# A two-block transformer kernel on one core: norms by token halves, unread products at the opening and in the last norm, and low halves sooner

## The reference, cut to what matters

```
first_block:  h = rmsnorm(x);  proj = h @ w_in             # compressed, selected, window attention
              mix = concat(o_nsa, o_swa) @ w_o
              x = x + rmsnorm(mix)                         # "y1": the norm behind w_o
              h = rmsnorm(x);  y = (gelu(conv(a)) * u) @ w_down    # a, u = split(h @ w_gate_up)
              x = x + rmsnorm(y)                           # "y2": the norm behind w_down
              x = x + (p @ w_ple) * sigmoid(x @ w_ple_gate)
second_block: proj = rms_norm(x) @ w_in_2
              na  = neighbourhood_attention(q, k, v)       # 8 heads, softmax over a window
              ret = head_group_norm(bidirectional_retention(rotary(q), rotary(k), v))
              x = x + concat(na, silu(g) * ret) @ w_out_2
              x = x + square(relu(rms_norm(x) @ w_up_2)) @ w_down_2
result:       rms_norm(x)                                  # "x5": the last norm
```

## Time and profile before

| | us |
|---|---|
| three runs | 1301.70, 1303.32, 1304.52 |
| median | 1303.32 |
| the profiled execution | 1304.54 |
| its span, first to last instruction | 1302.7 |
| outside of the span | 1.8 |
| mean granted TensorE clock | 0.995 |

### The profile page before, as it was taken

The page is one execution under the profiler, slowest core; times in us unless marked ns, Lnnn a source line. Parts: engine busy times, 40 slices in busy tenths (PEclk is TensorE's granted clock), DMA queues, the critical chain, the costliest instruction groups (busy, mean ns, idle before and its releaser), DMA issues.

```text
span 1302.7 us, 16590 instructions
## 1 busy us (share of the span) xinstructions
PE 1278.1 (98%) x6086; PEld 1062.3 (82%) x6086; DVE 802.3 (62%) x1553; ACT 634.5 (49%) x1239; POOL 155.1 (12%) x146
## 2 busy tenths in 40 slices
PE   8999999999999999999999999999999999999997
PEld 7888888868888888888788777888888888888886
DVE  5789799685654566346788886588644343344344
ACT  6687576454335443233455655476543242332343
POOL 0021120000010001000002101022311030110111
PEclk9999999999999999999999999999999999999998
DMA  7211110423332333332333222432333323233321
GB/s 266 85 46 41 42 41 18 157 76 90 99 97 71 115 104 97 98 90 81 113 90 89 89 57 64 128 105 77 91 96 97 94 76 114 81 113 97 98 81 65
DMA packets 64623, 118.19 MB, mean 91 GB/s; under 512 B 7712, under 2 KB 12192, under 8 KB 64288
## 3 DMA queue, kind: packets, MB, share of 16 engines
q1 hardware_dynamic: 62848, 112.95, 29.2%
q10 hardware_dynamic: 1696, 4.19, 1.0%
HBM read 115.02 MB, written 2.10 MB: 90 GB/s over the span
## 4 chain that ended last, share of the span: by engine, by line
PE 88%; DVE 7%; ACT 2%; issue 2%; DMA 1%; POOL 0%; SPq 0%; POOLq 0%; DVEq 0%; ACTq 0%
PE bank L581 26%; PE bank L583 26%; PE bank L582 25%; PE bank L781 2%; PE bank L662 2%; PE bank L664 2%; PE bank L663 2%; DVE pp L2094 1%; PE bank L767 1%; PE bank L768 1%; DVE ptl L2117 1%; DVE pp L2111 1%; PE bank L735 1%; DMA praw<-in_pT 0%; DVE qs L2010 0%
## 5 line engine op out<-in xcount | busy, mean ns | idle before, releaser
L1923 DVE TENSOR_TENSOR wl<-raw,wh 128x512 fp32r<-128x512 f32 (+2 forms) x360 | 265.9, 750 | 330.8 <-ACT wh L1257 330.1
L1257 ACT ACTIVATE wh<-raw 128x512 fp32r<-128x512 f32 (+1 forms) x398 | 242.3, 619 | 289.6 <-PE bank L583 276.0
L581 PE MATMUL bank<-AH,wh 128*128 128x512 f32 (+1 forms) x848 | 333.5, 393 | 0.9 <-DVE AL L1937 0.3
L583 PE MATMUL bank<-AH,wl 128*128 128x512 f32 (+1 forms) x848 | 329.2, 388 | 0.0
L582 PE MATMUL bank<-AL,wh 128*128 128x512 f32 (+1 forms) x848 | 326.9, 386 | 0.0
L581 PE MATMUL bank<-BH,wh 128*128 128x512 f32 x624 | 247.9, 397 | 1.3 <-DVE wl L1923 1.3
L583 PE MATMUL bank<-BH,wl 128*128 128x512 f32 x624 | 244.7, 392 | 0.0
L582 PE MATMUL bank<-BL,wh 128*128 128x512 f32 x624 | 243.2, 390 | 0.0
L583 PEld LDWEIGHTS bank<-AH,wl 128*128 128x128 f32 x848 | 159.3, 188 | 35.4
L581 PEld LDWEIGHTS bank<-AH,wh 128*128 128x128 f32 x848 | 159.8, 188 | 34.7 <-issue 4.1
L582 PEld LDWEIGHTS bank<-AL,wh 128*128 128x128 f32 x848 | 159.5, 188 | 33.1 <-issue 0.2
(11 more groups left out here) (317 smaller groups left out, 1627.0 us busy)
## 6 DMA issues: line engine op xcount, KB each, us to landing
raw<-in_w_dn SPq DMA_DIRECT2D x104, 256.0 KB, 2.7
raw<-in_w_gu SPq DMA_DIRECT2D x88, 256.0 KB, 2.6
raw<-in_w_up SPq DMA_DIRECT2D x64, 256.0 KB, 2.6
raw<-in_w_nsa SPq DMA_DIRECT2D x16, 256.0 KB, 2.7
raw<-in_w_pg SPq DMA_DIRECT2D x16, 256.0 KB, 2.6
raw<-in_w_naq SPq DMA_DIRECT2D x16, 256.0 KB, 2.6
nbi<-in_na_bias ACTq DMA_DIRECT2D x8, 448.0 KB, 3.4
raw<-in_w_swa SPq DMA_DIRECT2D x10, 256.0 KB, 2.7
```

Source lines behind the costliest of these rows:

```text
L581: t.matmul(o, w, xh, start=start, stop=False, skip_group_check=skip)
L583: return t.matmul(o, wl, xh, start=False, stop=stop, skip_group_check=skip)
L1257: a.activation(W[i % NW].h[:, 0:n], RAW[i % NRAW][:, 0:n], ACT.Copy).then_inc(*s_wh.up(i))
L1923: v.tensor_tensor(w.l[:, 0:n], RAW[i % NRAW][:, 0:n], w.h[:, 0:n], ALU.subtract).then_inc(*s_wl.up(i))
```

## The change

1. Opening. The DMA of `cst` moves from SP's queue to ACT's, as its first instruction. PE begins with eight f32 products of `ones` by `ones`, 128 columns each, into a bank whose content is overwritten and never read. The 12 products of chunk 0 are put in another order, with a wait for each kind: four w.h by x.h (after `AH` and `wh`), four by x.l (after `AL`), four w.l (after `wl`).
2. Norms y1 and y2. The last chunk is added in two halves of 256 tokens (`y1_last`, `y2_last`), squared in two (`squares_by_halves`), and PE's sums of it wait for each half apart. Chunk 0 is scaled, added and split to `AH` in halves (`x1_first`, `x2_first`, `first_split`), and PE's fresh products take half the columns at a time. ACT loads the root's table earlier: in y1 two chunks sooner, in y2 during the last down products. In y1 `behind("w_ple", 0)` moves behind the first chunk's scaling and adding.
3. Retention. On DVE two low halves of `w_ret` (behind 3, ahead 4) move ahead of rotated_low(0) and rotated(1).
4. Neighbourhood attention. On DVE rest(s-2) goes before soft(s) in every round.
5. Last norm. On ACT last_root(0) goes before last_square(6, 1); on DVE last_norm(0) before last_add(6, 1). PE gets three f32 products of `ones` between the two sources of last_sums(1) and six behind it, into a bank of their own, not read.

The diff, cut to its core; products within are shown by their first line where they repeat:

```diff
@@ tokens
+                for n in range(warm):
+                    t.matmul(bs[3][:, 0:P], ones[:, :], ones[:, :], start=True, stop=True)
...
+                    if warm and k == 0:
+                        e.wait_ge(s_xh.at(("x0", 0)), s_wh.at(i))
+                        for b in range(4):
+                            t.matmul(bs[b][:, 0:N], x.h[:, P * b:P * b + P], w.h[:, 0:N], start=True, stop=False)
+                        e.wait_ge(ready(0))
...
+                        e.wait_ge(low(i))
...
@@ product, fresh
-                        e.wait_ge(s_xh.at((fresh, ks[0])))
...
+                        for h in range(2):
+                            o = of_tokens(h)
+                            e.wait_ge(s_xh.at((fresh, ks[0], h)))
...
@@ squares_of
+                    if halves and i % 2 == 0:
+                        e.wait_ge(s_sq.at((key, 7, i // 2)))
@@ last norm on PE
+                    if n and h:
+                        awake(3)
...
             last_sums(1)
+            awake(6)
@@ ACT
+            a.dma_start(cst[:, 0:c_used[0]], ins["consts"]).then_inc(*s_c.up("in", by=16))
...
             for c in range(8):
+                if c == 6:
+                    root_table("y1")
                 hi(WHERE["w_o_nsa", c] + 4)
...
-                if c == 7:
-                    root_table("y1")
-                out1(c)
+                if c < 7:
+                    out1(c)
+            squares_by_halves("y1", chunk(ACC, 7), ("y1", 7))
...
+                        if j == 6:
+                            root_table("y2")
...
-            root_table("y2")
-            down_out(2, 7)
+            squares_by_halves("y2", chunk(ACC, 7), ("dn", 2, 7))
...
+            last_root(0)
             last_square(6, 1)
-            last_root(0)
@@ DVE
+            def x1_first(h):
+                v.scalar_tensor_tensor(out=t[:, o], in0=chunk(ACC, 0)[:, o], ...
+                v.tensor_tensor(chunk(X, 0)[:, o], chunk(X, 0)[:, o], t[:, o], ALU.add)...
...
+            x1_first(0)
+            x1_first(1)
             behind("w_ple", 0)
-            x1_scaled(0)
-            x1_sum(0)
...
-            x2_scaled(0)
-            x2_sum(0)
+            x2_first(0)
+            x2_first(1)
...
             rotated(0)
+            behind("w_ret", 3)
+            ahead("w_ret", 4, 2)
             rotated_low(0)
             rotated(1)
-            behind("w_ret", 3)
-            ahead("w_ret", 4, 2)
...
             for s in range(10):
+                if s >= 2:
+                    u = s - 2
+                    rest(NA, ("na", u), PT2[u % 2], ...
                 if s < 8:
                     soft(NA, ("na", s), PP2[s % 2], ...
-                if s >= 2:
-                    u = s - 2
-                    rest(NA, ("na", u), PT2[u % 2], ...
...
+            last_norm(0)
             last_add(6, 1)
-            last_norm(0)
@@ SP
-            d.dma_start(cst[:, 0:c_used[0]], ins["consts"]).then_inc(*s_c.up("in", by=16))
```

More of the change, by code:

```diff
@@ L583, in triple, with group @@
                 return t.matmul(o, wl, xh, start=False, stop=stop, skip_group_check=skip)
-            def group(name, k, bs, keys, src, ready, ks, first, last):
+            def group(name, k, bs, keys, src, ready, ks, first, last, skip=False):
                 G = len(keys)
@@ L1222, in last_sums, with awake @@
                 bank.give(("st", "x5", h))
+            def awake(n):
+                for _ in range(n):
+                    t.matmul(bank.ap(("awake",))[:, 0:P], ones[:, :], ones[:, :], start=True, stop=True)
             def last_back(name, h):
@@ L1238, in tensor @@
             last_part(7, 1, {(0, 2): lambda: last_back("bk", 0), (1, 0): lambda: last_back("bk2", 0)})
+            b, free = bank.take(("awake",))
+            e.wait_ge(*free)
             last_sums(1)
+            awake(6)
+            bank.give(("awake",))
             last_back("bk", 1)
@@ L1278, in square, with squares_by_halves, first_split @@
                         sqr.read((key, c), (s_st, (key, "c", c)))
+            def squares_by_halves(key, x, done):
+                for h in range(2):
+                    e.wait_ge(s_sv.at((*done, h)), *sqr.before((key, 7)))
+                    a.activation(sqr.ap((key, 7))[:, of_tokens(h)], x[:, of_tokens(h)], ACT.Square).then_inc(*s_sq.up((key, 7, h)))
+                sqr.read((key, 7), (s_st, (key, "c", 7)))
+            def first_split(key, dst, src, scale, *ready):
+                for h in range(2):
+                    o = of_tokens(h)
+                    e.wait_ge((s_sv if key == "x1" else s_dv).at((key, 0, h)), *ready)
+                    if scale is None:
+                        m = a.activation(dst.h[:, o], src[:, o], ACT.Copy)
+                    else:
+                        m = a.activation(dst.h[:, o], src[:, o], ACT.Copy, scale=scale)
+                    m.then_inc(*s_xh.up((key, 0, h)))
             def root(key):
@@ L2248, in y1, with y1_last @@
                 bank.read(key, (s_sv, ("y1", c)))
+            def y1_last():
+                key = ("wo", 7)
+                e.wait_ge(s_mm.at(("o", key)), s_cp.at(("wos", 7)), s_pv.at(N_UNITS - 1))
+                for h in range(2):
+                    o = of_tokens(h)
+                    v.tensor_tensor(chunk(ACC, 7)[:, o], bank.ap(key)[:, o], ACC1[7][:, o], ALU.add).then_inc(*s_sv.up(("y1", 7, h)))
+                bank.read(key, (s_sv, ("y1", 7, 1)))
             for c in range(8):
-                y1(c)
+                if c < 7:
+                    y1(c)
+                else:
+                    y1_last()
                 behind("w_o_nsa", c)
```

94 lines of the change are left out of this document (65 added, 29 removed).

## The result

| | before | changed |
|---|---|---|
| median of 13 runs | 1302.19 | 1305.15 |
| lowest to highest | 1301.50 to 1304.75 | 1302.72 to 1307.27 |
| profiled execution's span | 1302.7 | 1305.5 |

The ratio is 1.0017, with a 95% interval of 1.001 to 1.0025: slower by 2 to 3 us, where I had forecast 1297.2 and given "slower" a chance of 0.04. By my own bound of 0.2% it is "within 0.2%", but it lies outside of the range and on the wrong side of the old kernel.

A forecast was written before the change was run, and what follows sets the result against it. PE, busy 98% of 1302.7 us, was taken as the bound. Terms 2.6 + 2.3 + 0.2 + 1.1 - 1.5 + 2.0 = 6.7 us gave 1297.8 from the profiled run, 1296.6 from the median; forecast 1297.2, range 1293.5 to 1301.0.

The forecast's parts named there:

- Neighbourhood, -1.5 forecast: Neighbourhood attention: values start no sooner, exp 1.6 later, loop 7.4 us against PE's 6.85; loss 1.5, bounds +1.6 and -2.5.
- Carried through the last four rounds ... earlier rounds add some tenths: Neighbourhood attention: the longer loop ends the stage 1.1 us later over four rounds, earlier rounds adding some tenths.
- Rival (d): Neighbourhood rounds, 842 to 905 us: waits lower the clock, 1.7 a fall, six falls giving 1307.4; chance 0.04.
- Opening, 2.6 forecast: Start of kernel: first product at about 5.1, clock up sooner through unread products; gain 2.6 us, bounds 1.3 and 3.1.
- the rise again 5.6 us after the first real product: Opening, lower bound: unread products do nothing for the clock, gain 1.3 us.
- Norm y1, 2.3 forecast: Norm y1: sums end 0.7 sooner and the half clock behind them goes; gain 2.3 us, bounds 0.6 and 2.4.
- If the clock stays up: Norm y1, behind the sums: PE reaches L711 at 266.8, a gain of 2.4 us; if it falls again, 0.7.
- Norm y2, 0.2: Norm y2: sums 0.5 sooner, DVE pays 0.28 more for halves; gain 0.2 us, bounds 0 and 0.5.
- Retention, 1.1 forecast: Retention: PE's wait of 1.31 for `wl` goes entirely; gain 1.1 us, bounds 0.8 and 1.5.
- about 0.5 of room: Retention: rotated low halves come some 0.6 later; products using them, 10 us on, have about 0.5 us of room.
- Last norm, 2.0: Last norm: 1.5 from the wait for identity blocks, 0.5 from spreading at full clock; bounds 1.3 and 2.4.
- the two clock terms: The gains forecast for the opening (2.6) and norm y1 (2.3), together 4.9 of 6.7 us.

The follow-up runs named there:

- b_na_new: The kernel before with only the neighbourhood order changed, rest(s-2) before soft(s): 1309.00 us, ratio 1.0053.
- a_na_late: The changed kernel with rest(s-2) before soft(s) only in neighbourhood rounds 6 to 9, which project nothing: 1298.78 us, ratio 0.9971.
- b_open10: The kernel before with only the opening changed, with ten unread products instead of eight: 1298.95 us, ratio 0.9971.
- a_na_old: The changed kernel with soft(s) before rest(s-2) again in all ten neighbourhood rounds: 1297.79 us, ratio 0.9961.
- n_ret_old: The changed kernel with the neighbourhood order and the retention order undone: 1298.39 us, ratio 0.9967.

## Why the prediction was wrong, step by step

- **Neighbourhood, -1.5 forecast, about -7 measured (7.4 in the changed kernel, 6.4 in the old).** This is the step that put the time outside of the range. The mechanism named was right: PE gained nothing from `p2l` sooner, exp came later, and the loop took 7.35. What failed is its size. The failing step is "Carried through the last four rounds ... earlier rounds add some tenths". I had worked out only rounds without projections, where the loop costs 0.8; the rounds with them, taken at some tenths, cost 6.9. In the earlier ones ACT's conversions stand behind exp too, and DVE's instructions on them slid into POOL's. In the old order they missed one another narrowly: POOL's ended at 868.17, DVE's began at 868.18. I looked at who waits for whom, and not at what else runs when a group moves by 1.6 us.
- **Rival (d)** had the place and the clock, and 0.04. Its first half came true once, not six times: one wait of 2.7, and 6.8 us at half clock behind it. What it lacked was the cause that makes a wait this long.
- **Opening, 2.6 forecast, 1.0 in the trace.** The lower bound, "the rise again 5.6 us after the first real product", was nearly it: the products start at 5.69 instead of 5.1 and the clock rose at 10.2. Three steps failed. That all from `xin` on comes 0.43 sooner: `AH` starts no sooner with the constants on ACT's queue (4.23 to 4.67) than on SP's (4.22 to 4.40). That eight unread products help: they brought the clock early in three profiles of nine, which the medians don't show; ten brought it early both times (1 to 2 us in the median). And that the old opening has 5.6 us between its first product and the rise: in b_na_new, with the same opening, the clock rose at 9.5 instead of 12.0, 2.9 us behind the first product, and this put it 1.0 ahead of the old trace. I had taken a single profile's stretch for a fixed one.
- **Norm y1, 2.3 forecast.** The sums ended 0.7 sooner as forecast, but the clock fell here too (262.8 to 266.2):

```profile
260.50 1.08 PE L712 MATMUL bank<-ones,r_bc 128*128 128x64 f32 x8 [1.00 <-DVE r_bc L2047]
261.41 1.06 PE L712 MATMUL bank<-ones,sqr 128*128 128x64 f32 x8
...
266.70 1.05 PE L731 MATMUL bank<-tmp,ones 128*128 128x128 f32 x8
```

  Against the earlier trace rows the wait of 0.66 has shrunk to 0.2 and 0.60 has become 1.00. From the first sum to `w_gu` the halves are worth 0.8 with or without a fall: so it is from b_na_new to a_na_late, where neither fell, and from b_open10 to a_na_old, where both did. But the longer wait ahead of the first sum takes from it, 0.4 in the table, 0.2 and 0.9 in these two pairs, so that of y1 0.4, 0.6 and nothing are left. The fall itself comes and goes: 3 of 11 profiles with the new norm, 2 of 3 with the old. That the new norm makes it rarer stays open. It was a term that a single profile couldn't carry, and I put it in whole: the step that failed is "If the clock stays up", 1.7 of the 2.3.
- **Norm y2, 0.2:** right, 0.17. PE's wait for the squares fell from 0.70 to 0.22, and what DVE's halves cost took the rest.
- **Retention, 1.1 forecast, 0.35.** The wait moved, as the price "about 0.5 of room" foresaw, but it came back as 1.2 ten us on, not as the 0.2 that 1.1 out of 1.31 left for it. ACT and DVE hand the rotated halves to and fro, and that chain started at the same distance from its entrance as before: DVE filled its wait of 0.70 and had one of 0.71 for ACT right after. What is left is 0.1 in the changed kernel's trace and 0.4 against n_ret_old.
- **Last norm, 2.0:** right in sum, 1.9 to 2.1, of which 1.5 is the order, seen in the lead of a_na_old over b_open10 at L1231; the share of the unread products was not settled.
- **The sum without the neighbourhood** was 8.2; a_na_old measures 4.9. With ten unread products it is 7. So even without the neighbourhood the kernel won 3 us less than I had added up, through the two clock terms and retention.

## What to carry to other kernels

Moving a group of instructions moves all that runs beside it: before such a move list, for the two engines that share a path to SBUF, which of their instructions now overlap, in every kind of round and not in the simplest. A wait taken from PE is won only as far as the chain behind it has slack, so look for the next wait ten us on. Eight unread products won nothing and ten won 1 to 2 us, and no profile says why: try such a number in several runs. A stretch at half clock in one profile isn't a property of the kernel; before its end is counted as a gain, look for it in a second profile.

## What the runs showed of the hardware

DVE's instructions on two operands in SBUF wait out POOL's. In the old kernel's own trace, `wl<-raw,wh` of 128x512 takes 0.689 us on the mean where POOL is idle (304 times) and 1.390 where it overlaps one of POOL's by 0.1 us or more (33 times), and ends some 0.5 after POOL's. POOL's keep their 1.3, but for one of 1.74 that began at 811.59 while a `wl` of DVE's ran. With a bank as an operand nothing happens: `X<-X,bank` takes 0.688 (37 times) and 0.685 beside POOL (9 times). The Trainium skill says this ("SBUF — State Buffer", SBUF: two separate sides): the pair of ports that DVE and GpSimd share is locked for a whole instruction, for DVE by one with two SBUF inputs against a GpSimd instruction that reads SBUF, and the other side blocks. By that rule, which the trace before already bore out, the change had a price that I didn't look for.
